# Two-block kernel: first loads in halves, shorter reciprocal roots, a bias table laid by 128 transfers

## What is computed

```python
x = _layernorm(ALPHA * x + y, ln_w[layer], ln_b[layer])        # end of each layer of the first block
...
mod = c_act @ w_ada[l] + b_ada[l]                              # c_act = silu(c)
h = rms_norm(x, norm1_w[l]) * (1.0 + sc1) + sh1                # start of the second block
proj = h @ w_in[l]
...
bias = rpb[:, rr, rc].astype(jnp.float32)                      # neighbourhood attention: a bias by relative position
s = jnp.einsum('bqhd,bqnhd->bhqn', qblk, kb).astype(jnp.float32) * scale + bias[None]
...
return rms_norm(x, final_w)
```

## Time and profile before

| what | us |
|---|---|
| median of three runs | 2251.86 |
| lowest and highest | 2249.84, 2254.5 |
| the profiled execution, its own time | 2254.25 |
| its span from first to last instruction | 2252.6 |
| TensorE busy | 2209.9 (98% of the span) |
| VectorE busy | 1501.2 (67%) |
| ScalarE busy | 1010.7 (45%) |
| the 16 DMA engines, mean rate | 222 GB/s |

### The profile page before, as it was taken

How to read it: one execution, slowest core, us unless ns; L and a number is a source line. 1 busy time by engine, 2 the same in 40 slices (tenths; PEclk the granted TensorE clock), 3 DMA queues, 4 the chain that set the end, 5 groups by cost and what they waited for, 6 DMA issues and landing times.

```text
span 2252.6 us, 32553 instructions
## 1 busy us (share of the span) xinstructions
PE 2209.9 (98%) x10948; PEld 1868.6 (83%) x10948; DVE 1501.2 (67%) x2021; ACT 1010.7 (45%) x1232; POOL 229.9 (10%) x430
## 2 busy tenths in 40 slices
PE   8999999999999999999999999999999999999997
PEld 6898878988887778899888888888888888888886
DVE  5766668877766878688776767765665656454544
ACT  4445544554444434433565443444443444443433
POOL 1101111012210011001101110110100110000000
PEclk9999999999999997999999999989999999999999
DMA  8768577678885584768756876755777676565563
GB/s 275 233 177 249 160 254 252 190 228 276 313 280 175 160 299 152 245 189 262 226 184 186 289 259 218 236 199 185 258 234 237 221 257 213 179 215 182 187 200 131
DMA packets 198881, 499.21 MB, mean 222 GB/s; under 512 B 30717, under 2 KB 58077, under 8 KB 198629
## 3 DMA queue, kind: packets, MB, share of 16 engines
q1 hardware_dynamic: 167236, 394.74, 54.5%
q0 software_dynamic: 31520, 102.78, 13.8%
HBM read 495.34 MB, written 2.10 MB: 221 GB/s over the span
## 4 chain that ended last, share of the span: by engine, by line
PE 87%; DVE 5%; DMA 3%; ACT 2%; issue 2%; SPq 1%; POOLq 0%; DVEq 0%; ACTq 0%; POOL 0%
PE ps L2000 71%; PE ps L2038 10%; DMA ada_raw<-in_w_ada_dram 2%; DVE lo L1110 1%; PE ps L2246 1%; ACT hi L631 1%; PE ps L2398 1%; PE ps L2388 1%; PE ps L2065 0%; DMA xT_raw<-in_xT_dram 0%; DVE acc_s L1122 0%; PE ps L2469 0%; PE ps L2076 0%; SPq L442 0%; DVE acc_g L1122 0%
## 5 line engine op out<-in xcount | busy, mean ns | idle before, releaser
L1110 DVE TENSOR_TENSOR lo<-raw,hi 128x1024 fp32r<-128x1024 f32 x732 | 891.7, 1223 | 575.6 <-ACT hi L631 573.3
L631 ACT CAST hi<-raw 128x1024 fp32r<-128x1024 f32 x732 | 763.9, 1051 | 1014.0 <-PE ps L2000 786.4
L2000 PE MATMUL ps<-hi,XH 128*128 128x512 f32 x1952 | 618.5, 397 | 18.5 <-DVE lo L1110 14.1
L2000 PE MATMUL ps<-lo,XH 128*128 128x512 f32 x1952 | 607.4, 391 | 0.0
L2000 PE MATMUL ps<-hi,XL 128*128 128x512 f32 x1952 | 605.5, 390 | 0.0
L2000 PEld LDWEIGHTS ps<-hi,XH 128*128 128x128 f32 x1952 | 361.4, 189 | 95.6 <-issue 13.5
L2000 PEld LDWEIGHTS ps<-lo,XH 128*128 128x128 f32 x1952 | 368.0, 189 | 78.1
L2000 PEld LDWEIGHTS ps<-hi,XL 128*128 128x128 f32 x1952 | 367.6, 188 | 78.4
L559 POOL DMA_DIRECT2D ada_raw<-in_w_ada_dram x384 | 206.8, 539 | 1583.6 <-DVE acc_s L1122 970.9
L1122 DVE SCALAR_TENSOR_TENSOR acc_s<-ada_raw,c_act,acc_s 128x512 f32<-128x512 f32 x256 | 191.1, 747 | 13.2 <-DMA ada_raw<-in_w_ada_dram 12.4
L2038 PE MATMUL ps<-XH,hi 128*128 (+1 forms) x512 | 145.0, 283 | 0.0
(11 more groups left out here) (344 smaller groups left out, 1820.0 us busy)
## 6 DMA issues: line engine op xcount, KB each, us to landing
ada_raw<-in_w_ada_dram POOLq DMA_DIRECT2D x384, 256.0 KB, 4.6
raw<-in_w_in_dram SPq DMA_DIRECT2D x136, 512.0 KB, 4.4
raw<-in_ml_w_in_dram SPq DMA_DIRECT2D x128, 512.0 KB, 4.7
raw<-in_w_gate_dram SPq DMA_DIRECT2D x176, 256.0 KB, 3.0
raw<-in_w_up_dram SPq DMA_DIRECT2D x176, 256.0 KB, 3.5
raw<-in_w_down_dram SPq DMA_DIRECT2D x88, 512.0 KB, 4.4
raw<-in_mla_w_in_dram SPq DMA_DIRECT2D x48, 512.0 KB, 4.5
raw<-in_mla_w_out_dram SPq DMA_DIRECT2D x32, 512.0 KB, 4.5
```

The costliest lines, as they stand in the source:

```text
L631: nc.scalar.copy(hi[:, j, :], raw[:, j, :]).then_inc(hi_ready, 1)
L1110: nc.vector.tensor_tensor(lo[:, j, :], raw[:, j, :], hi[:, j, :].bitcast(F32), ALU.subtract) \
L2000: ins = mm(ps[:, o:o + HALF], x, w[:, b % RING, c0:c0 + HALF], start=first, stop=(k == n_rows - 1 and x is xl), skip_group_check=True)
```

## The change

It has six parts.

1. **First loads.** `xT` is loaded in five parts of 2, 2, 4, 4 and 4 chunks, the first weight block in two halves of 512 columns, and the later parts of `xT` between the blocks. ACT and DVE split in that order. TensorE starts on the first half (`first_block`), and before that runs nine 128x128 products of ones.
2. **Angles and c_act.** The angle steps become hooks between the blocks of the first product; `c_act` moves behind the first four blocks of the second product.
3. **Roots.** `rsqrt(n=1)` has seven instructions in place of nine.
4. **Bias table.** The products, their copies, `toep` and the rounding of `rel` go. GpSimd clears `na_bias` (eight memsets), two loads bring `rel` into partitions 0 and 64, and SP lays each query's 16 columns with one transfer of 3 KB from SBUF to SBUF, eight after each of the 16 weight blocks of `B_QB`.
5. **Between the blocks.** The last pass over tile 1 is cut in two, ACT squares it in halves, `modulation` comes before the second root, and the second half of tile 1 is scaled on ACT. At the end of the first layer ACT scales the rows before it copies `mods`.
6. **The end.** The last scaling and the last stores of tile 1 go in halves.

```diff
             def load_x(q):
-                sp.dma_start(xT_raw[:, 4 * q:4 * q + 4, :], xT_v[:, 4 * q:4 * q + 4, :]).then_inc(ev(f"xT{q}"), 16)
+                sp.dma_start(xT_raw[:, x_part(q), :], xT_v[:, x_part(q), :]).then_inc(ev(f"xT{q}"), 16)
...
                     for j in range(RING):
                         dst, src = source(j, j)
-                        sp.dma_start(dst, src).then_inc(w_landed[j], 16)
-                    for q in range(1, 4):
-                        load_x(q)
-                    first = 1
+                        if j == 0:
+                            sp.dma_start(dst[:, 0:HALF], src[:, 0:HALF]).then_inc(ev("w0_half"), 16)
+                            sp.dma_start(dst[:, HALF:COLS], src[:, HALF:COLS]).then_inc(w_landed[j], 16)
+                        else:
+                            sp.dma_start(dst, src).then_inc(w_landed[j], 16)
+                        if j == 1:
+                            load_x(1)
+                    for j in range(RING, nb):
+                        if j % RING == 0:
+                            load_x(j // RING + 1)
+                        dst, src = source(j, j % RING)
+                        sp.wait_ge(lo_ready, j - RING + 1)
+                        sp.dma_start(dst, src).then_inc(w_landed[j % RING], 16)
+                    return
...
-                    sp.wait_ge(ev("rel_zero"), 1)
-                    for part in range(2):
-                        load("rel", rel[64 * part:64 * part + 31, :, :], rpbT[:, :, 5:11])
-                        load("rel", rel[64 * part + 32:64 * part + 63, :, :], rpbT[:, :, 4:10])
+                    for half in range(2):
+                        load("rel", rel[GRID_W * half:GRID_W * half + 1, :, :, :],
+                             rpbT[:, :, 5 - half:5 - half + REL_R].unsqueeze(0))
...
-            for q in range(3):
+            def bias_window(b):
+
+                if b == 0:
+                    sp.wait_ge(ev("rel"), 32)
+                    sp.wait_ge(ev("bias_zero"), 8)
+                for qc in range(4 * b, 4 * b + 4):
+                    first = min(max(qc - NA_COLS // 2, 0), GRID_W - NA_COLS)
+                    j = first - qc + NA_COLS - 1
+                    for half in range(2):
+                        p = GRID_W * half
+                        load("bias", na_bias[p + qc:p + qc + 1, first:first + NA_COLS, :, :],
+                             rel[p:p + 1, j:j + NA_COLS, :, :])
+
+            blocks(B_QB, 16, w, 1536, bias_window)
+            for q in range(1, 3):
                 stream(B_QB + 16 * q, 16, plain(w, 1536 + q * COLS))
...
-            nc.gpsimd.memset(rel[:, :, :], 0.0).then_inc(ev("rel_zero"), 1)
+            for c0 in range(0, GRID_W, 8):
+                nc.gpsimd.memset(na_bias[:, c0:c0 + 8, :, :].rearrange("p c h i -> p (c h i)"), 0.0) \
+                  .then_inc(ev("bias_zero"), 1)
...
-            whole("ada1a", mods[:, 0, :], width=16)
             act.wait_ge(ev("shift_col"), 1)
             norm_first(0)
+            whole("ada1a", mods[:, 0, :], width=16)
...
+                    unit = (256.0 / 3.0) ** 2
+                    link(nc.vector.tensor_scalar(a, src, unit * scale, unit * EPS, ALU.mult, ALU.add))
+                    link(nc.vector.tensor_scalar(y.bitcast(I32), a.bitcast(I32), -0.5, 1597463007.0 - 2 ** 31,
+                                                 ALU.mult, ALU.add))
+                    link(nc.vector.scalar_tensor_tensor(out=t, in0=y, scalar=a, in1=y, op0=ALU.mult, op1=ALU.mult))
+                    link(nc.vector.scalar_tensor_tensor(out=y, in0=t, scalar=3.0, in1=y, op0=ALU.subtract,
+                                                        op1=ALU.mult))
+                    link(nc.vector.scalar_tensor_tensor(out=t, in0=y, scalar=a, in1=y, op0=ALU.mult, op1=ALU.mult))
+                    link(nc.vector.scalar_tensor_tensor(out=t, in0=t, scalar=40.0 / 3.0, in1=t, op0=ALU.subtract,
+                                                        op1=ALU.mult))
+                    ins = nc.vector.scalar_tensor_tensor(out=y, in0=t, scalar=80.0, in1=y, op0=ALU.add, op1=ALU.mult)
...
             x2_rows(1)
             rms_token(0, 1, ss[:, 0:1])
-            rms_token(1, 2, ss[:, 1:2])
-            normalise_second()
+            modulation("ada1", "norm1", False)
+            dve.wait_ge(ev("first_squares"), 1)
+            rms_token(1, 2, None)
+            normalise_second(1)
             lo_block(B_QA, 0)
-            modulation("ada1", "norm1", False)
...
             pe.wait_ge(ev("ones"), 1)
-            token_major("c", B_C, 16, XH, XL, lambda k: (ev("x_lo"), k // 4 + 1))
+            o = grp("z1")
+            for _i in range(9):
+                mm(ps[:, o:o + P], ones[:, :], ones[:, :], start=True, stop=True, skip_group_check=True)
+            for b in range(2):
+                first_block(start("c"), b)
+            token_major("c", B_C, 16, XH, XL, lambda k: (ev("x_lo"), k // 2 + 1 if k < 4 else k // 4 + 2),
+                        blocks=(2, 16))
```

More of the change, by code:

```diff
@@ L1280, in _ @@
-            left = 2 * np.pi
-            src = ang
-            for part in range(4):
-                c = float(np.float32(left))
-                if part < 3:
-                    e = int(np.floor(np.log2(left)))
-                    c = float(np.floor(left / 2.0 ** (e - 7)) * 2.0 ** (e - 7))
-                left -= c
-                link(nc.vector.scalar_tensor_tensor(out=rot[:, :, :], in0=turns_n[:, :, :], scalar=-c, in1=src[:, :, :],
-                                                    op0=ALU.mult, op1=ALU.add))
-                src = rot
@@ new lines, in angle_turns, with angle_rests @@
+            def angle_turns():
+                link(nc.vector.tensor_scalar(turns_n[:, :, :], ang[:, :, :], 1.0 / (2 * np.pi), magic, ALU.mult,
+                                             ALU.add))
+                link(nc.vector.tensor_scalar(turns_n[:, :, :], turns_n[:, :, :], magic, None, ALU.subtract))
+            def angle_rests(parts):
+                left = 2 * np.pi
+                for part in range(4):
+                    c = float(np.float32(left))
+                    if part < 3:
+                        e = int(np.floor(np.log2(left)))
+                        c = float(np.floor(left / 2.0 ** (e - 7)) * 2.0 ** (e - 7))
+                    left -= c
+                    if part in parts:
+                        link(nc.vector.scalar_tensor_tensor(out=rot[:, :, :], in0=turns_n[:, :, :], scalar=-c,
+                                                            in1=rot[:, :, :] if part else ang[:, :, :], op0=ALU.mult,
+                                                            op1=ALU.add))
@@ L1677, in rms_token, with normalise_second @@
                 rsqrt(1, 1.0 / D, src, ev("rms"), at=tok)
-            def normalise_second():
-                for half in range(2):
+            def normalise_second(n):
+                for half in range(n):
                     cols_ = slice(half * COLS, (half + 1) * COLS)
@@ L2355, in _ @@
             token_major("qa", B_QA, 16, XH, XL, h_tiles, blocks=(0, 5))
-            for tok in range(TOK):
-                pe.wait_ge(ev(f"h_norm{tok}"), 2)
+            pe.wait_ge(ev("h_norm0"), 2)
+            pe.wait_ge(ev("h_norm1_rest"), 1)
             transposes("hTb", operand_tiles(h_norm, 8))
@@ L2509, in shape_constants @@
     put("window", np.where((kc >= start) & (kc < start + NA_COLS), 0.0, NEG))
-    toep = np.zeros((64, 191))
-    for half in range(2):
-        for j in range(REL_C):
-            toep[32 * half + j, GRID_W * half + 78 - j] = 1.0
-    put("toeplitz", np.tile(toep, (2, 1)))
     inv = (np.float32(10000.0) ** (-np.arange(0, HD // 2, 2, dtype=np.float32) / (HD // 2))).astype(np.float32)
```

212 lines of the change are left out of this document (114 added, 98 removed).

## The result

The changed kernel takes 2282.16 us (median of four runs, 2280.97 to 2283.57), the kernel before 2252.09 in the same comparison: a ratio of 1.0132 (95% interval 1.0119 to 1.0144). Forecast were 2242.9 us and a range up to 2255.0. The forecast is wrong in sign, and rival (b) is what happened, at its price though not by its mechanism.

A forecast was written before the change was run, and what follows sets the result against it. TensorE, busy for 98% of the span, was taken as the bound. Terms of -4.6 +1.4 -1.0 -0.8 -2.7 -1.3 + 0 = -9.0 us took 2251.9 to 2242.9 us, with a range of 2239.5 to 2255.

The forecast's parts named there:

- rival (b): B_QB: a transfer within single partitions costs SP 0.66 us apart, giving 2278 us, or 2420 at 1.79; chance 0.10.
- The 128 transfers: B_QB, nine transfers issued by SP per weight block: delay 0, bounds 0 and +12.1 us.
- p: B_QB: time from one small issue to the next on SP, taken as 0.38 us; 0.48 for issues in a row.
- The count of engines as a sign: B_QB: 31 partitions go to one engine, 16 lines to all, so the new transfers are of the fast kind.
- The start: First product: smaller first loads and products of ones let block 2 start at 11.8 us; -4.6, bounds -2.5 and -5.
- the table load: Second product: moved with c_act out of ACT's spare time, it lengthens TensorE's 0.41 us stall; +1.4 us.
- the landing of weight block 1: First product: with parts of 256 KB, block 1 lands at 7.1 us by bytes.
- End of the first layer: TensorE's transposes: ACT scales some 3 us earlier, so 1.49 us of idling go; -1.0, bounds -0.5 and -1.4.
- Beside lo1: Two `rel` loads in place of four and no `toep` give back TensorE's stalls; -0.8 us, bounds 0 and -1.2.
- Between the blocks: From lo1 to qa: shorter roots and one scaling on ACT start qa earlier; -2.7 us, bounds -2 and -3.2.
- The tail: End of the kernel: two shorter roots and last scalings in halves; -1.3 us, bounds -0.9 and -1.6.
- Before the feed-forward part: The chain there is TensorE's own one-column products, so two shorter roots give 0.

The follow-up runs named there:

- the probe: The kernel before with 70 more transfers into unused memory, in ten groups, each behind one weight block of B_QB or B_KB; 2251.39 us beside 2253.71 of before.
- spread version: The changed kernel with the same 128 transfers, three after each weight block of B_QA, B_QB and B_KB in place of eight in B_QB; 2245.98 us, ratio 0.9967.

## Why the prediction was wrong, step by step

**The 128 transfers: the step that failed.** The model was right. SP's issues per block against TensorE's 2.86 us per block, 16 x (0.38 + 8p) + 945.7 - 1001.1, gives 31.3 us for the measured p of 0.63. The measured 34.7 differ because the weight's issue right behind a small one is 0.58 and not 0.34: with 0.63 + 0.54 + 7 x 0.63 + 0.1 = 5.68 for a block, the formula gives 35.5. Wrong was p, 0.38, and worse, its upper bound in the range, 0.48. Both came from the earlier trace rows, where every transfer comes out of HBM. No row of the trace showed a transfer from SBUF to SBUF. I took the nearest rows for the same kind, and their pace in a row as the upper bound. The text had the slope, 128 us per us of p, so an error of 0.1 us in p was worth 12.8 us, more than the whole sum; and rival (b) named 0.66 and 2278 us, 4 us below the result. That belongs inside a range when the price is unseen and the slope is so steep. It stood at 0.10 and outside.

The reason that I gave for a low p, that an issue's length is work on its lines and 16 lines are few, is refuted by the probe: 192 bytes, 3 KB in one piece and 128 partitions all cost the same 0.63 within SBUF. Rival (b)'s own reason, single partitions, is refuted too (0.29 from HBM).

**The count of engines as a sign.** From the Trainium skill, DMA: Bandwidth & Descriptors, "Why a DMA increments its semaphore by 16 and not by 1", I took the count of engines as a sign of a fast or slow issue, of which the section says nothing. The probe shows no such link within SBUF, where a single piece and 128 partitions take the same 0.59 us. The rule that did bear on the case is in another page of the Trainium skill, Perfetto Trace Analysis, "What 'DMA-bound' means": a kernel can be bound on the sequencer that issues, whose track is then solid transfers. SP's timeline above is that picture. The remedy that the section gives, larger descriptors, would not have helped: 3 KB in one piece was issued no faster than in 16. The fixed cost of 2.0 us per transfer, which the prediction cited and set aside, did not count, as the prediction says: the 128 landed a median of 2.1 us after their issue, and DVE first used the table more than 60 us after the last of them had landed.

**The start.** Forecast -4.6 at the end of the first product and +1.4 for the table load. Measured -2.2 (52.9 us in place of 55.1, from the start of the stall and four blocks of 2.72 us before it), +1.5, and +1.6 of half pace on top. The table load was sized right. That a longer stall can bring half pace was written for the end of the first layer and for qa and not for this stall. Two terms failed in the first product. One is the half pace after TensorE's stop of 1.63 us; without it block 2 started at 12.7 to 13.6 us in the five other kernels with the halves, the products of ones and early small loads. The other is the landing of weight block 1, 7.1 us by bytes. It landed at 8.2 to 9.7 us in the seven kernels with halves and GpSimd's loads at the same time, at 7.5 and 8.5 with halves and late small loads, and at 7.04 with neither. The one profile of whole blocks with late small loads agrees with the sum by bytes. The small loads cost 0.5 us in the old start, and the earlier trace rows had shown a sign of it: block 1 stood 1.80 us behind block 0 there, and the sum took the mean of 1.53. How much is due to the halves and how much to the small loads in the new start, single profiles can't say, and no run has whole blocks and early small loads in the new order.

**End of the first layer**: forecast -1.0. Measured -0.9 from the last product before it to the end of the transposes (8.55 us in place of 9.41). The idling is 0.6 of it, 1.49 us having become 0.26 and 0.64; the one-column products just before were shorter too, 3.87 us in place of 4.53. The size was right, the mechanism for two thirds of it.

**Beside lo1**: forecast -0.8. Not to be told. From the start of lo0 to the end of lo1 it is 95.6 us before and 95.8 after; among the kernels of the experiments 94.3 to 95.7 with the new loads and 95.4 to 98.2 with the old. The issues of `rel` did fall, from 1.79 us to a median of 0.75. The stretch before it, from 378 us to lo0, where no part of the change edits anything, took 389.4 to 392.4 us in different kernels, and 1.9 us more in the changed kernel than in the one before. That is as large as the smaller terms; its cause stays open.

**Between the blocks**: forecast -2.7, measured -2.9 against the one profile of the kernel before and -2.3 against two others of the same code. The steps held: a root is 1.47 us long (863.22 to 864.69), ACT's third scaling is queued, qa starts 19.5 us after lo1. What was not seen is that this depends on the table's products being gone, which the text priced at 0.

**The tail**: forecast -1.3, measured -1.1. **Before the feed-forward part**: forecast 0; the first product there was 1.3 us shorter, by a shorter stretch of half pace. The same happened at qa, 1.9 us. Neither was forecast, and neither is shown to come from the change: the kernel before with late small loads, whose code at both places is the old one, was 1.1 and 1.9 us shorter there than the profile of the kernel before.

Without the transfers' price, the sum was -9.0. The spread version, which has all of the change but that price, measured -7.4 (0.9967 of 2252). So the other terms together were good to 1.6 us, and one was off by 35. That the sum came so near is partly luck. In its profile the spread version is 3.0 us ahead of the kernel before at qa, where -7.7 was forecast, and 8.3 at the end; after qa only 1.3 were forecast, and most of the other 4 are the stretches of half pace that differ between profiles of the same code.

## What to carry to other kernels

Before you hang small transfers on the queue that feeds the weights, write down issues per block times pitch and compare it with the consumer's time per block; if the trace has no row of that kind of transfer, take the slowest issue on the page as the bound, and spread them until even that fits. Ask of each "covered" piece of work whether it is still covered in the order that the change makes. And judge a smaller first load by what all queues move at that time, not by its own bytes: here the second half of a block landed later than the whole block did. Before a gain of 1 or 2 us in one profile is put down to an edit, look at the same stretch in a second profile of the same code.

## What the hardware showed that I had not expected

- SP issues a transfer from SBUF to SBUF in 0.59 us (0.63 apart) in all five forms tried, from 192 bytes in one piece to 128 partitions; from HBM to 16 or 128 partitions, or from SBUF to HBM, in 0.42 to 0.45 (0.47 apart); 3 KB from HBM into one partition in 0.25 (0.29 apart).
- The issue behind it pays too: a weight load takes 0.33 us after a pause, 0.36 right behind one-partition loads from HBM, and 0.58 right behind an issue within SBUF.
- The second half of one weight block, issued 0.5 us after the first, landed 1.3 to 3.0 us after it, in nine profiles.
- The stretch of half pace behind a pause differs between executions of the same instructions: with it the time from qa to B_QB is 69.3 us in one profile of the old code and 67.3 in two others.
